# Row gates of a two-block transformer kernel: three of four spread over the partitions by DMA instead of by matmuls

## The reference

```python
c_act = jax.nn.silu(c)
for i in range(DEPTH):
    mod = c_act @ w_mod[i] + b_mod[i]
    sh1, sc1, g1, sh2, sc2, g2 = jnp.split(mod, 6, axis=-1)
    h = modulate(rmsnorm(x, norm_mix[i]), sh1, sc1)
    y = pool_mixer(...) if i % N_MIXERS == 0 else moba_attention(...)
    x = x + g1[:, None, :] * y
    h = modulate(rmsnorm(x, norm_mlp[i]), sh2, sc2)
    x = x + g2[:, None, :] * squared_relu_mlp(h, w_up[i], w_down[i])
```

## Time and profile before

| | |
|---|---|
| median of 3 runs | 1144.57 us (1140.43 to 1145.12) |
| profiled execution, device time | 1144.98 us |
| its span in the trace | 1143.3 us |
| mean granted TensorE clock | 0.91 |
| TensorE matmul busy | 1023.0 us (89%) |
| VectorE busy | 647.6 us (57%) |
| ScalarE busy | 461.2 us (40%) |
| GpSimd busy | 116.1 us (10%) |
| DMA, mean over the span | 171 GB/s |

### The profile page before, as it was taken

How to read it: one execution, slowest core, us unless ns; L and a number is a source line. 1 busy time by engine, 2 the same in 40 slices (tenths; PEclk the granted TensorE clock), 3 DMA queues, 4 the chain that set the end, 5 groups by cost and what they waited for, 6 DMA issues and landing times.

```text
span 1143.3 us, 16537 instructions
## 1 busy us (share of the span) xinstructions
PE 1023.0 (89%) x6589; PEld 901.3 (79%) x6589; DVE 647.6 (57%) x1003; ACT 461.2 (40%) x747; POOL 116.1 (10%) x109
## 2 busy tenths in 40 slices
PE   3779999997997798899999789999579689999996
PEld 1459899986996586898998689977468569999995
DVE  1466777687547965645544566432744545554554
ACT  2344344444344222544444445542311434443443
POOL 2012011130000000111111100020443000000000
PEclk8889999999997659899999889985679899999999
DMA  9997677876365662255455433620000123555520
GB/s 324 372 387 275 237 256 250 290 268 240 129 234 191 238 221 74 104 192 189 178 204 184 148 132 127 220 74 1 1 1 1 38 74 111 191 176 186 202 89 37
DMA packets 105186, 195.60 MB, mean 171 GB/s; under 512 B 2283, under 2 KB 46572, under 8 KB 105132
## 3 DMA queue, kind: packets, MB, share of 16 engines
q1 hardware_dynamic: 104380, 192.58, 47.7%
q0 software_dynamic: 752, 2.26, 0.6%
HBM read 193.76 MB, written 1.07 MB: 170 GB/s over the span
## 4 chain that ended last, share of the span: by engine, by line
PE 78%; DVE 12%; ACT 3%; DMA 3%; issue 2%; POOL 1%; SPq 0%; DVEq 0%; POOLq 0%; ACTq 0%
PE ps L1686 27%; PE ps L1704 15%; PE ps L1940 7%; PE ps L2148 5%; PE ps L1632 4%; PE ps L1827 4%; DMA raw<-in_w_mod 3%; DVE wl L1072 2%; DVE accu L975 2%; PE ps L2079 1%; ACT arena L585 1%; PE ps L2090 1%; POOL x L450 1%; PE ps L2089 1%; PE ps L1854 1%
## 5 line engine op out<-in xcount | busy, mean ns | idle before, releaser
L1072 DVE TENSOR_TENSOR wl<-raw,wh 128x1024 fp32r<-128x1024 f32 (+1 forms) x288 | 315.5, 1138 | 266.6 <-ACT wh L568 266.6
L568 ACT ACTIVATE wh<-raw 128x1024 fp32r<-128x1024 f32 (+1 forms) x288 | 268.4, 982 | 352.4 <-PE ps L1686 188.1
L1686 PE MATMUL ps<-H,wh 128*128 128x256 f32 x864 | 245.4, 284 | 5.4 <-DVE L L1055 4.4
L1686 PE MATMUL ps<-H,wl 128*128 128x256 f32 x864 | 245.5, 284 | 0.0
L1686 PE MATMUL ps<-L,wh 128*128 128x256 f32 x864 | 245.1, 284 | 0.0
L1686 PEld LDWEIGHTS ps<-H,wh 128*128 128x128 f32 x864 | 166.0, 192 | 9.2 <-issue 8.1
L1686 PEld LDWEIGHTS ps<-L,wh 128*128 128x128 f32 x864 | 166.1, 192 | 0.0
L1686 PEld LDWEIGHTS ps<-H,wl 128*128 128x128 f32 x864 | 165.4, 191 | 0.9
L1704 PE MATMUL ps<-wh,aTh 128*128 128x512 f32 x256 | 101.8, 398 | 1.6 <-DVE wl L1072 1.6
L1704 PE MATMUL ps<-wl,aTh 128*128 128x512 f32 x256 | 101.2, 395 | 0.0
L1704 PE MATMUL ps<-wh,aTl 128*128 128x512 f32 x256 | 101.1, 395 | 0.0
(11 more groups left out here) (378 smaller groups left out, 1716.8 us busy)
## 6 DMA issues: line engine op xcount, KB each, us to landing
raw<-in_w_up SPq DMA_DIRECT2D x16, 2048.0 KB, 8.7
raw<-in_w_down SPq DMA_DIRECT2D x16, 2048.0 KB, 7.7
raw<-in_w_mod SPq DMA_DIRECT2D x12, 2048.0 KB, 16.0
raw<-in_w_in SPq DMA_DIRECT2D x7, 2048.0 KB, 7.7
raw<-in_w_mod SPq DMA_DIRECT2D x12, 1024.0 KB, 7.1
raw<-in_w_qkv SPq DMA_DIRECT2D x6, 2048.0 KB, 11.2
raw<-in_w_mod SPq DMA_DIRECT2D x8, 1536.0 KB, 7.0
raw<-in_w_gate SPq DMA_DIRECT2D x11, 1024.0 KB, 5.3
```

Of the source, the lines that this page charges most:

```text
L568: e.activation(dst, src, ACT.Copy).then_inc(S["split_h"], 1)
L1072: e.tensor_tensor(o, src, i1.bitcast(F32), ALU.subtract).then_inc(S["split_l"], 1)
L1686: ins = e.matmul(ps[:, 4 + b, SEQ * c:SEQ * c + SEQ], w[wb][:, k, P * c:P * c + P], (H, L)[xa][:, k, META:TT], start=(k == 0 and n == 0), ...
```

## The change

The gates g2 of layer 0, g1 and g2 of layer 1 no longer pass through diagonals, matmuls and copies. GpSimd stores the gate's 128x8 block of `modc` to a row of 1024 floats in DRAM (`gate_store`, 4 bytes at a time, with a stride of 128 floats from column to column), waits for it, and loads the row to all 128 partitions (`gate_load`). The residuals wait for `gate_in` (16 for each load) instead of `gate_set`. Store 0 stands in GpSimd's program behind `squares(2)`, load 0 behind `squares(3)`, and both pairs of layer 1 behind the first MLP's residual. TensorE's wait for `r_done` moves behind the last `down`.

```diff
+        gate_rows = nc.dram_tensor("gate_rows", [3, D], F32).ap()
...
+            def gate_store(i, l, col, ready):
+                e.wait_ge(S["mod_col"], ready)
+                e.dma_start(gate_rows[i].rearrange("(r p) -> p r", p=P), modc[:, l, col:col + 8],
+                            allow_slow_non_contiguous=True).then_inc(S["gate_out"], 16)
+
+            def gate_load(i, dst):
+                e.wait_ge(S["gate_out"], 16 * (i + 1))
+                e.dma_start(gate[dst][:, :], gate_rows[i].partition_broadcast(P)).then_inc(S["gate_in"], 16)
+            squares(1)
+            squares(2)
+            gate_store(0, 0, 40, 12)
+            squares(3)
+            gate_load(0, 1)
+            with e.Fori(4, 8) as j:
                 squares(j)
             residual()
+            gate_store(1, 1, 16, 18)
+            gate_load(1, 0)
+            gate_store(2, 1, 40, 19)
+            gate_load(2, 1)
             residual()
...
-            gate_diag(modc[:, 0, 40:48])
...
-            gate_copy(1, 4)
...
-            residual(1, 4, [(y, 3), (y, 4), (y, 5), (used, 2 * (T_MLP0 + 16))], then=normalise_tile)
+            residual(1, (S["gate_in"], 16), [(y, 3), (y, 4), (y, 5), (used, 2 * (T_MLP0 + 16))], then=normalise_tile)
...
-            gate_diag(modc[:, 1, 16:24])
-            gate_copy(0)
-            gate_diag(modc[:, 1, 40:48])
-            gate_copy(1)
             split_h()
             split(T_WO + 1, landed(N_WO + 1)[0])
...
+            down(7, 1, T_MLP0 + 15, last=True, between=lambda: mods_layer1(7, 1))
             e.wait_ge(S["r_done"], 16)
-            gate_mm(4)
-            down(7, 1, T_MLP0 + 15, last=True, between=lambda: mods_layer1(7, 1))
-            e.wait_ge(S["gate_set"], 4)
             e.wait_ge(S["mod_col"], 18)
...
             feature_major([(S["o_ev"], 4)] * 2)
-            gate_mm()
-            e.wait_ge(S["gate_set"], 6)
-            gate_mm()
-            e.wait_ge(S["gate_set"], 8)
             fresh[0] = 12
             wo_out(T_WO)
```

More of the change, by code:

```diff
@@ L216, in build @@
             cpad_z cpad_set mod_rd mod_chain mod_acc mod_mm mod_col split_h split_l split_used
-            gate_diag gate_mm gate_set mods_set f_mm f_sb
+            gate_diag gate_mm gate_set gate_out gate_in mods_set f_mm f_sb
             sq_done rstd_done xn_done tr_done hf_done hs_h hs_l sc_chain
@@ L465, in _ @@
                         ).then_inc(S["tb_in"], 16)
-            with e.Fori(1, 8) as j:
+            def gate_store(i, l, col, ready):
[11 more added lines that the diff above has]
+            with e.Fori(4, 8) as j:
                 squares(j)
             residual()
+            gate_store(1, 1, 16, 18)
+            gate_load(1, 0)
+            gate_store(2, 1, 40, 19)
+            gate_load(2, 1)
             residual()
@@ L1074, in _, with residual @@
             nr = [0]
-            def residual(g, gs, done, b=0, then=None):
+            def residual(g, made, done, b=0, then=None):
                 i = nr[0]
                 nr[0] += 1
-                e.wait_ge(S["gate_set"], gs)
+                e.wait_ge(*made)
                 def gated(m, c):
@@ L1151, in _ @@
             used, y = S["split_used"], S["y_done"]
-            residual(0, 2, [(y, 1), (y, 2), (used, 2 * T_POOL + 1), (used, 2 * T_POOL + 2)], b=4)
+            residual(0, (S["gate_set"], 2), [(y, 1), (y, 2), (used, 2 * T_POOL + 1), (used, 2 * T_POOL + 2)], b=4)
             normalise()
@@ L1265, in _ @@
             e.wait_ge(S["o_ev"], 4)
-            gate_diag(modc[:, 1, 16:24])
-            gate_copy(0)
-            gate_diag(modc[:, 1, 40:48])
-            gate_copy(1)
             split_h()
             split(T_WO + 1, landed(N_WO + 1)[0])
-            residual(0, 6, [(y, 6), (y, 7), (used, 2 * T_WO + 2), (used, 2 * T_WO + 4)], then=normalise_tile)
+            residual(0, (S["gate_in"], 32), [(y, 6), (y, 7), (used, 2 * T_WO + 2), (used, 2 * T_WO + 4)], then=normalise_tile)
             split(T_MLP1, landed(N_MLP1)[0], cols=True, qs=(0, 1))
@@ L1296, in _ @@
             e.reciprocal(stat[0:META, 2, NM:NM + 1], stat[0:META, 1, NM:NM + 1]).then_inc(S["sqm_done"], 1)
-            residual(1, 8, [(y, 8), (y, 9), (y, 10), (used, 2 * (T_MLP1 + 16))], then=first_output)
+            residual(1, (S["gate_in"], 48), [(y, 8), (y, 9), (y, 10), (used, 2 * (T_MLP1 + 16))], then=first_output)
             normalise()
```

## The result

| | before | changed |
|---|---|---|
| median of 20 runs | 1146.28 us (1137.94 to 1148.28) | 1138.75 us (1136.49 to 1140.93) |
| profiled execution, device time (span) | 1144.98 us (1143.3) | 1140.14 us (1138.4) |
| TensorE matmul busy | 1023.0 us | 1025.2 us |
| VectorE busy | 647.6 us | 639.2 us |

The ratio (changed over before) is 0.9946, 95% interval 0.9932 to 0.996: 6.2 us faster (4.6 to 7.8), where 7.6 was forecast. It was reckoned down from 1144.57, the median of three runs; over 20 runs the median before is 1146.28.

The account below looks back on a forecast made before the run. TensorE's matmul side, busy 1023.0 of 1143.3 us, was taken as the bound, so only its waits or needless work could save time. Savings of 1.8 + 5.8 = 7.6 us from 1144.57 gave 1137.0 us, range 1133.5 to 1141.5.

Parts of the forecast that it names:

- Part 1: End of the first MLP: gate matmuls ahead of the last `down` leave TensorE, saving 1.8 us; lower bound 1.3.
- the sum of 7.6: Whole kernel: 1.8 us at the first MLP plus 5.8 before `wo_out`, giving 1137.0 us; chance 0.56.
- Part 2: Between attention and `wo_out`: gate matmuls, copies and waits go, saving 5.8 us; low bound 5.2.
- The store: GpSimd's gate stores land in 7 us, hidden; rival: over 19.4 us delays the second residual's add, chance 0.05.
- The upper bound of 13.9: Longest landing allowed for a gate store, taken from a 2 MB load in 2048 pieces; leaves 5 us of cover.
- The 19 times of the Trainium skill: Slow-store estimate from a rule on rearranged DMAs: 19 times 4.9 us is 93 us, time some 1210 us.
- The collision: First MLP: gate load delays `w_up` and stalls TensorE 1.4 us, perhaps as much in QKV; 1138.4 to 1139.8; chance 0.08.
- The clock: Rival at `wo_out` or QKV: a later clock rise costs 1.85 us, so 5.8 saved, 1138.8; chance 0.15.
- the gate matmuls at the low clock: Before `wo_out`: late clock rises had hit the old gate matmuls, so 9.4 us saved, 1135.2; chance 0.08.

Follow-up runs that it names:

- e1: Only g2 of layer 0 through DRAM, layer 1's gates the old way, against the kernel before: ratio 1.0011 (0.9985 to 1.0037), median 1146.11 us.
- e8: The kernel of e1 timed once more against the kernel before: ratio 1.0008 (0.9981 to 1.0035), median 1145.68 us.
- e0: The changed kernel itself, run again as a control against the kernel before: ratio 0.995 (0.9926 to 0.9973), median 1138.19 us.
- e4: The whole change, but g1 of layer 1 made the old way, against the kernel before: ratio 0.9963 (0.9941 to 0.9984), median 1140.13 us.
- e7: The change, but layer 1's gates by old matmuls moved behind halves of the first `wo_out` tile, against the kernel before: ratio 0.9972, median 1141.84 us.
- e2: Only layer 1's two gates through DRAM, the first MLP's gate the old way, against the kernel before: ratio 0.9959 (0.9939 to 0.998), median 1141.67 us.
- e5: The change with stores as 128 pieces of 32 bytes (output differs), against the kernel before: ratio 0.994 (0.9915 to 0.9964), median 1137.93 us.
- e6: The change with layer 1's g2 stored three times, each waiting for the last, against the kernel before: ratio 1.0036 (1.0011 to 1.0062), median 1148.11 us.
- e9: The kernel before against itself, also for a second profile of it: ratio 1.0002 (0.9975 to 1.0029).

## Why the prediction was right, step by step

**Part 1, 1.8 us.** Its place shows 1.78, in all ten profiles without those matmuls, and so does the way to the residual's add (18.78 us for 20.56). All quarters were in time, and VectorE was still idle for 1.35 us before `mod_cols1(7)` (before: 1.94). That it reaches the end is not shown: e1 and e8, the two timings of this part alone, speak against it. This stays open, and with it whether the sum of 7.6 was right or only near.

**Part 2, 5.8 us.** Measured 5.64 on TensorE's side and 5.6 as a mean with the clock in it. Cast to first matmul took 428.65 - 427.35 = 1.30 us (forecast 1.29). The 0.2 us less than forecast lie between eviction and cast: 427.35 - 426.57 = 0.78 us, where 0.61 had been reckoned. TensorE did not starve behind it, as forecast: the 48 take 11.38 us in e0, as before. e4 and e7 show that both the matmuls and the waits around them were the price.

**The store, the mis-sized term.** Forecast 7 us to landing, from the 32-byte load of `wsm`; it is 10.3 to 12.4, and up to 13.6 in e2. e5 shows that this is the price of the 1024 small pieces: as 128 pieces of 32 bytes the same bytes land in 1.7 to 5.6. The upper bound of 13.9 just held, and so did the cover, with 10.1 us left in the changed kernel's first profile and 7.8 in e0's, where 12 had been reckoned. e6 shows what lies behind the cover. The 19 times of the Trainium skill (DMA: Bandwidth & Descriptors, "Rules for kernel authors"), taken over to this store as 93 us, did not show: the largest landing in any profile was 13.6.

**The collision.** Forecast up to 1.35 us of delay for `w_up`, against 1.5 of margin. ScalarE and VectorE at that tile of the changed kernel, against the earlier trace rows:

```profile
168.40 2.01 ACT L587 ACTIVATE wh<-raw 128x1024 fp32r<-128x1024 f32 x2 [5.18 <-DMA raw<-in_w_up]
...
169.50 2.36 DVE L1091 TENSOR_TENSOR wl<-raw,wh 128x1024 fp32r<-128x1024 f32 x2 [0.64 <-ACT wh L587]
```

Measured from the start of that `down` (160.76 us here, 156.37 before), ScalarE gets the tile after 168.40 - 160.76 = 7.64 us, before after 163.92 - 156.37 = 7.55: 0.1 us later. The load was issued at 163.73, and its bytes show: in the 2.3 us from 166.0 on the DMA engines moved 323 GB/s, where before, at the same distance from the `down` (from 161.6 on), they moved 117. The difference is 0.47 MB, about the 512 KB of the load. It hardly delayed `w_up`. TensorE was busy throughout, and nothing stalled.

**The clock.** It was held as a rival with 0.15, at 1.85 us, as a rise that comes a little later and falls into `wo_out`. That is what happened in the first profile, at 2.26 us, and in e2 and e5. The old kernel loses a like amount in e9 and e8, by a fall in `wo_out` and by gate matmuls at the low clock, and so the difference of the means is 5.6 all the same. That the sum could leave the clock out is luck in part: the prediction names the gate matmuls at the low clock (as a gain, with 0.08), but has no step for the old kernel's falls in `wo_out`. The rival's saving of 5.8 us is as much within the measured 4.6 to 7.8 as the sum's 7.6; the timed ratio does not decide between them, and no single term is shown to be the cause of the difference between 7.6 and 6.2.

## What to carry to other kernels

A row that is known early and used late can go through DRAM at nearly no cost, if the queue that stores it has nothing due before the store has landed: write down who stands behind the waiting instruction and how long it is idle, since past that point the wait goes into the kernel's time (10 us for two stores more in e6). Before taking matmuls away, look at what stands behind them in the other engines' programs: e7 gained about half by taking `split_h` out from behind the copies, with the matmuls still there. And single profiles of equal kernels can differ by more than the change; a stretch in its place tells more, and a timed ratio decides.

## What the runs showed of the hardware that was not expected

The 500 us behind the second MLP have the same instructions in every kernel here, and yet took from 493.8 to 502.4 us, from GpSimd's first add there to the end. The two profiles of the kernel before differ there by 3.7 us (641.84 to 1143.3, and 647.38 to 1145.1). It arises in the forgetting attention of the second block, where TensorE runs short groups of two to four small matmuls (64 columns in many of them). Windows of before and of e9 there, and ScalarE's first eviction behind it in each:

```profile
776.30:791.80 15.50, 15.50 (x64) 11.84 (x63) 4.25 (x19) 4.95 (x19) 0.00 (x0) 0.50 0.01 2
```

```profile
807.81 1.09 ACT L803 ACTIVATE v_t<-ps 128x512 f32<-128x512 f32 x2 [10.82 <-PE ps L2022]
```

```profile
781.80:794.00 12.20, 12.20 (x67) 9.22 (x67) 4.25 (x19) 4.95 (x19) 0.00 (x0) 0.73 0.01 2
```

```profile
809.23 1.09 ACT L803 ACTIVATE v_t<-ps 128x512 f32<-128x512 f32 x2 [11.24 <-PE ps L2022]
```

Once the granted clock stays at 0.50 throughout, once it is up for part of the time, and the stretch from the add to that eviction is 165.97 and 161.85 us. The Trainium skill (TensorE: Matmul & The Clock Gate, "HAM oscillation — how this bites in real kernels") tells of kernels whose clock falls in waits for DMAs and rises again with the next burst of matmuls. The clock falls and rises here too, but no such wait is seen: in both windows TensorE counts as busy for the whole time (15.50 of 15.50 us, 12.20 of 12.20), and still stands at the low level for 15.5 us in one of them. What decides the level here was not tested. Nor was whether this is why runs of one kernel differ: of the 20 runs of before 16 lie at 1144 to 1148 us and four below 1141, a gap that the changed kernel's runs don't show.
